# Mean norms: TensorE adds the last tile's sum and square, the mean is spread in two products, and GpSimd makes weight pieces ahead of rescaled tiles

## The reference

```python
def layer_norm(x, g, b):
    mu = jnp.mean(xf, axis=-1, keepdims=True)
    var = jnp.mean(jnp.square(xf - mu), axis=-1, keepdims=True)
    return (xf - mu) * lax.rsqrt(var + LN_EPS) * g + b

# second_block, l = 0, 1
h = modulate_2(x, sh1, sc1)
y = short_conv_mixer(h, ...) if l == 0 else forgetting_attention(h, ...)
x = layer_norm(DEEPNORM_ALPHA * x + g1 * y, ln1_g[l], ln1_b[l])    # n4 (l = 0), n6 (l = 1)
h = modulate_2(x, sh2, sc2)
y = swiglu(h, w_gate[l], w_up[l], w_down[l])
x = layer_norm(DEEPNORM_ALPHA * x + g2 * y, ln2_g[l], ln2_b[l])    # n5 (l = 0), n7 (l = 1), the output
```

## Time and profile before

| what | us |
|---|---|
| three runs: median (lowest to highest) | 1933.12 (1932.42 to 1933.66) |
| the profiled execution | 1932.42 |
| its span, first to last instruction | 1930.6 |
| TensorE busy | 1875.5 (97%) |
| VectorE, ScalarE, GpSimd busy | 1407.1, 853.5, 438.7 |
| mean granted TensorE clock | 0.992 of full |

### The profile page before, as it was taken

How to read it: one execution, slowest core, us unless ns; L and a number is a source line. 1 busy time by engine, 2 the same in 40 slices (tenths; PEclk the granted TensorE clock), 3 DMA queues, 4 the chain that set the end, 5 groups by cost and what they waited for, 6 DMA issues and landing times.

```text
span 1930.6 us, 25635 instructions
## 1 busy us (share of the span) xinstructions
PE 1875.5 (97%) x10248; PEld 1614.1 (84%) x10248; DVE 1407.1 (73%) x2157; ACT 853.5 (44%) x1296; POOL 438.7 (23%) x379
## 2 busy tenths in 40 slices
PE   6999999999999999999999999999999999999997
PEld 4788888878888887888789999977899778999996
DVE  7777665567766766776768787986677776877797
ACT  5677532352222225222534333457677553433343
POOL 4323111021111113001411121135634141112212
PEclk9999999999999999999999999999999999999998
DMA  9622366357667652753232323313221322332331
GB/s 333 163 81 72 127 220 239 109 197 260 242 241 258 242 194 62 297 187 130 67 105 94 107 89 109 110 66 135 67 66 44 98 77 89 108 107 91 109 100 54
DMA packets 142632, 267.76 MB, mean 139 GB/s; under 512 B 4576, under 2 KB 66032, under 8 KB 142513
## 3 DMA queue, kind: packets, MB, share of 16 engines
q1 hardware_dynamic: 137552, 248.59, 38.0%
q0 software_dynamic: 4960, 17.53, 2.6%
HBM read 261.84 MB, written 8.45 MB: 140 GB/s over the span
## 4 chain that ended last, share of the span: by engine, by line
PE 67%; DVE 5%; ACT 3%; POOL 2%; issue 2%; DVEq 0%; POOLq 0%; ACTq 0%
PE ps L739 21%; PE ps L741 21%; PE ps L740 21%; DVE t L1746 1%; DVE t L1798 1%; PE ps L899 1%; ACT t L1366 1%; ACT t L1362 1%; DVE t L1734 1%; PE ps L888 1%; PE ps L877 0%; POOL t L2630 0%; PE ps L916 0%; PE ps L917 0%; PE ps L915 0%
## 5 line engine op out<-in xcount | busy, mean ns | idle before, releaser
L739 PE MATMUL ps<-t 128*128 128x512 f32 (+1 forms) x2936 | 1026.3, 350 | 11.5 <-POOL t L2514 5.1
L741 PE MATMUL ps<-t 128*128 128x512 f32 (+1 forms) x2936 | 1020.1, 347 | 0.0
L740 PE MATMUL ps<-t 128*128 128x512 f32 (+1 forms) x2936 | 1016.6, 346 | 0.0
L739 PEld LDWEIGHTS ps<-t 128*128 128x128 f32 x2936 | 555.7, 189 | 85.0 <-issue 11.0
L741 PEld LDWEIGHTS ps<-t 128*128 128x128 f32 x2936 | 555.2, 189 | 72.1
L740 PEld LDWEIGHTS ps<-t 128*128 128x128 f32 x2936 | 555.5, 189 | 68.6 <-issue 1.0
L1734 DVE TENSOR_TENSOR t<-t 128x2048 fp32r<-128x2048 f32 x97 | 229.5, 2366 | 174.4 <-ACT t L1313 174.4
L1313 ACT ACTIVATE t<-t 128x2048 fp32r<-128x2048 f32 x97 | 185.3, 1910 | 328.6 <-PE ps L741 322.3
L1798 DVE SCALAR_TENSOR_TENSOR t<-ps,t 128x512 f32<-128x512 f32 x184 | 130.0, 746 | 68.1 <-PE ps L741 64.6
L1746 DVE CUSTOM_DVE_ANT_0 t<-t 128x1024 f32<-128x1024 f32 x144 | 168.8, 1220 | 3.6 <-DMA t<-in_ada 3.6
L2419 POOL TENSOR_TENSOR t<-t 128x512 fp32r<-128x512 f32 x88 | 115.4, 1329 | 195.1 <-ACT t L1320 194.4
(11 more groups left out here) (192 smaller groups left out, 1982.5 us busy)
## 6 DMA issues: line engine op xcount, KB each, us to landing
t<-in_ada SPq DMA_DIRECT2D x48, 1024.0 KB, 6.0
t<-in_gate SPq DMA_DIRECT2D x22, 1024.0 KB, 5.3
t<-in_up SPq DMA_DIRECT2D x22, 1024.0 KB, 5.3
t<-in_down SPq DMA_DIRECT2D x22, 1024.0 KB, 5.0
t<-in_w_in SPq DMA_DIRECT2D x17, 1024.0 KB, 6.2
t<-in_w_mlp_in SPq DMA_DIRECT2D x16, 1024.0 KB, 5.4
t<-in_w_mlp_out SPq DMA_DIRECT2D x16, 1024.0 KB, 5.1
t<-in_ada_t POOLq DMA_DIRECT2D x13, 1024.0 KB, 6.3
```

The source lines that it names most:

```text
L739: pe.matmul(o, wh, xh, start=first, stop=False)
L740: pe.matmul(o, wh, xl, start=False, stop=False)
L741: return pe.matmul(o, wl, xh, start=False, stop=last)
```

## The change

In each mean norm `sum7` and the addition of the last square are gone from VectorE. TensorE does both by accumulation: the products of `dsum` (tiles 0 to 6) and of tile 7 go to the same bank, and so do those of `acc` and of tile 7's square. The mean is spread by one product of `dsum` and one of tile 7 in bank 4 instead of 7. The centring of tile 0 moves ahead of the variance, so that two are left behind the reciprocal (in n7 three of four). In n5 the convert that stood ahead of the variance is cut in halves, one of them moved ahead of residual 6. In n3, n4 and n6 GpSimd's loop is split in two: the four pieces, then the eight rescaled tiles.

```diff
-                    on.wait_ge(acc, "dsum", site)
+                    on.wait_ge(p_sum, "dsum", site, 6)
                     for i, c in enumerate(blocks):
-                        ins = pe.matmul(psum[1][:, i:i + 1], m["dsum"][:, c], ones[:, 0:1], start=True, stop=True)
+                        pe.matmul(psum[1][:, i:i + 1], m["dsum"][:, c], ones[:, 0:1], start=i == 0, stop=False, ...)
+                    claim(4)
+                    pe.matmul(d[:, :], ones, m["dsum"], start=True, stop=False)
+                    on.wait_ge(acc, "acc", site, 6)
+                    for i, c in enumerate(blocks):
+                        pe.matmul(q[:, i:i + 1], m["acc"][:, c], ones[:, 0:1], start=i == 0, stop=False, ...)
+                    on.wait_ge(x_res, *last)
+                    for i, c in enumerate(blocks):
+                        ins = pe.matmul(psum[1][:, i:i + 1], X[7][:, c], ones[:, 0:1], start=False, stop=True, ...)
                     ins.then_inc(mm.sem, mm.up(site, "means"))
-                    on.wait_ge(acc, "acc", site, 7)
+                    pe.matmul(d[:, :], ones, X[7], start=False, stop=True).then_inc(mm.sem, mm.up(site, "mean"))
+                    on.wait_ge(a_norm, site, "sq", 7)
                     for i, c in enumerate(blocks):
-                        ins = pe.matmul(q[:, i:i + 1], m["acc"][:, c], ones[:, 0:1], start=True, stop=True)
+                        ins = pe.matmul(q[:, i:i + 1], m["sq"][0][:, c], ones[:, 0:1], start=False, stop=True, ...)
                     ins.then_inc(mm.sem, mm.up(site, "sums"))
-                    claim(7)
-                    pe.matmul(d[:, :], ones, m["dsum"], start=True, stop=True).then_inc(mm.sem, mm.up(site, "mean"))
...
             def roots(site, layer, *x_done):
                 if layer:
+                    centre(site, 0, *x_done)
...
-            sum7("n4", "co", 7)
-            add("n4", 7)
-            roots("n4", True)
+            roots("n4", True, x_res, "co", 0)
...
+                            if f == 5 and k == 5 and slot[0] < len(SLOTS):
+                                convert_half(slot[0], 0)
...
                 if slot[0] < len(SLOTS):
-                    convert(slot[0])
+                    convert_half(slot[0], 1)
...
             for k in range(KT):
                 next_piece(k)
+            for k in range(KT):
                 rescale("n4", "h4", k, cC, cD)
```

More of the change, by code:

```diff
@@ L821, in idle_products, with norm_finish @@
                     pe.matmul(psum[6][:, 0:256], ident, cst[:, 0:256], start=True, stop=True)
-            def norm_finish(site, layer, acc, rs_last):
+            def norm_finish(site, layer, acc, rs_last, *last):
                 m = norm_mem[site]
-                q, d, r = psum[3], psum[7], psum[5]
+                q, d, r = psum[3], psum[4], psum[5]
                 idle = site != "n1"
@@ L831, in norm_finish @@
                     claim(1)
-                    on.wait_ge(acc, "dsum", site)
+                    on.wait_ge(p_sum, "dsum", site, 6)
                     for i, c in enumerate(blocks):
-                        ins = pe.matmul(psum[1][:, i:i + 1], m["dsum"][:, c], ones[:, 0:1], start=True, stop=True)
+                        pe.matmul(psum[1][:, i:i + 1], m["dsum"][:, c], ones[:, 0:1], start=i == 0, stop=False,
+                                  skip_group_check=True)
+                    claim(4)
+                    pe.matmul(d[:, :], ones, m["dsum"], start=True, stop=False)
+                    on.wait_ge(acc, "acc", site, 6)
+                    for i, c in enumerate(blocks):
+                        pe.matmul(q[:, i:i + 1], m["acc"][:, c], ones[:, 0:1], start=i == 0, stop=False,
+                                  skip_group_check=True)
+                    on.wait_ge(x_res, *last)
+                    for i, c in enumerate(blocks):
+                        ins = pe.matmul(psum[1][:, i:i + 1], X[7][:, c], ones[:, 0:1], start=False, stop=True,
+                                        skip_group_check=True)
                     ins.then_inc(mm.sem, mm.up(site, "means"))
                     freed[1] = [(a_norm, (site, "squared"))]
-                    on.wait_ge(acc, "acc", site, 7)
+                    pe.matmul(d[:, :], ones, X[7], start=False, stop=True).then_inc(mm.sem, mm.up(site, "mean"))
+                    freed[4] = [(d_norm, (site, "centred", 7))]
+                    on.wait_ge(a_norm, site, "sq", 7)
                     for i, c in enumerate(blocks):
-                        ins = pe.matmul(q[:, i:i + 1], m["acc"][:, c], ones[:, 0:1], start=True, stop=True)
+                        ins = pe.matmul(q[:, i:i + 1], m["sq"][0][:, c], ones[:, 0:1], start=False, stop=True,
+                                        skip_group_check=True)
                     ins.then_inc(mm.sem, mm.up(site, "sums"))
-                    claim(7)
-                    pe.matmul(d[:, :], ones, m["dsum"], start=True, stop=True).then_inc(mm.sem, mm.up(site, "mean"))
-                    freed[7] = [(d_norm, (site, "centred", 7))]
                 else:
@@ L1167, in program_pe @@
             mm.also("end of h4")
-            norm_finish("n5", True, d_norm, "times")
+            norm_finish("n5", True, d_norm, "times", "dn", 0, 5, 7)
             at_end("pe", 5, mm)
@@ L1201, in program_pe @@
                         norm_shift("n6", 3, x_res, "op", 0)
-            norm_finish("n6", True, d_norm, "times")
+            norm_finish("n6", True, d_norm, "times", "op", 7)
             at_end("pe", 7, mm)
             ffn2(1, "n7", "h6")
-            norm_finish("n7", True, d_norm, "times")
+            norm_finish("n7", True, d_norm, "times", "dn", 1, 5, 7)
             at_end("pe", 8, mm)
@@ L1735, in convert, with convert_half @@
                     w_lo_d.sem, w_lo_d.up("slot", n))
+            def convert_half(n, half):
+                s = slice(1024 * half, 1024 * half + 1024)
+                on.wait_ge(w_hi, "slot", n)
+                ins = dve.tensor_tensor(WL[:, n % NW, s], raw[:, n % NRAW, s], WH[:, n % NW, s].bitcast(F), ALU.subtract)
+                if half:
+                    ins.then_inc(w_lo_d.sem, w_lo_d.up("slot", n))
             def ada_sum(j):
@@ L1822, in shift, with centre, roots @@
                         d_norm.sem, d_norm.up(site, "shifted", k))
-            def roots(site, layer):
+            def centre(site, k, *x_done):
+                on.wait_ge(mm, site, "mean")
+                on.wait_ge(*x_done)
+                dve.tensor_tensor(X[k], X[k], psum[4][:, :], ALU.subtract).then_inc(
+                    d_norm.sem, d_norm.up(site, "centred", k))
+            def roots(site, layer, *x_done):
                 v = col4[:, 0:4]
                 if layer:
+                    centre(site, 0, *x_done)
                     on.wait_ge(a_norm, site, "squared")
@@ L1841, in normed @@
             def normed(site, name, layer=False, tm=None, x_before=None):
[L1842 to L1846, removed]
                 if layer:
-                    for k in range(3):
-                        centre(k)
+                    for k in (1, 2):
+                        centre(site, k, *x_before(k))
                 on.wait_ge(mm, site, "rs")
@@ L1864, in normed @@
                     if layer and k + 3 < KT:
-                        centre(k + 3)
+                        centre(site, k + 3, *x_before(k + 3))
                     if name and k:
@@ L2394, in program_dve @@
             ffn2(1, "n7", 96, "n6", None)
[L2396 to L2403, removed]
+            for k in (1, 2, 5):
+                centre("n7", k, x_res, "dn", 1, 5, k)
             on.wait_ge(a_norm, "n7", "rs")
@@ L2408, in program_dve @@
                 if ahead:
-                    centre(ahead)
+                    centre("n7", ahead, x_res, "dn", 1, 5, ahead)
         def program_pool(pool, on):
```

15 lines of the change are left out of this document (3 added, 12 removed).

## The result

| | before | changed |
|---|---|---|
| runs: median (lowest to highest), us | 1933.86 (1932.42 to 1934.19) | 1942.16 (1941.27 to 1946.67) |
| the profiled execution, its span, us | 1932.42, 1930.6 | 1946.67, 1944.9 |
| mean granted TensorE clock | 0.992 | 0.987 |

A forecast was written before the change was run, and what follows sets the result against it. TensorE was taken to bound the kernel, with 67% of the chain. Norms and GpSimd's pieces in n3 to n7 plus 0.8 us for the clock gave +8.0 us, so 1941.1 us, range 1936.5 to 1945.5.

The forecast's parts named there:

- TensorE's list: In norms n4 to n7: with the added products, the variance comes 6.95 us behind the start of the idle products.
- What it gives back: In n4: the first normed tile follows the variance by 1.97 us instead of 2.69, which returns 0.72 us.
- GpSimd's tail: In n4 and n6: eight rescaled tiles behind the pieces take 8.55 us, so each norm costs +1.85 us.
- a wait at the third slot: In n4: TensorE waits about 1 us for VectorE's convert, 11 us later; no such wait would be wrong.
- The rival that kept the tail covered: Behind the norms: rescaled tiles run near 0.76 us and TensorE's own path counts; +5.4 us, 1938.5 us, chance 0.15.
- The price of the parts together: GpSimd's pieces ahead of the rescaled tiles: -0.2 us in n3, and 1.85 against 2.2 us in n4 and n6.
- The gain of the waits: TensorE's three waits for GpSimd's last piece go: 1.25 us gained in n4, 0.6 to 0.7 each in n3 and n6.
- The clock: In the four mean norms: more one-column products bring more falls to the 1.2 GHz level, +0.8 us together.
- The bound: In each mean norm: the most that falls of the clock were taken to cost, up to 1 us.
- The sum: Whole kernel: -0.2 (n3) + 1.85 (n4) + 1.4 (n5) + 1.85 (n6) + 2.3 (n7) + 0.8 (clock) = +8.0 us.
- One-column passes nearly free: Rival, in the mean norms: a one-column pass costs less than 0.05 us; -5 us, 1928 us, chance 0.05.

The follow-up runs named there:

- the second profile: The whole change run once more, unaltered, beside the kernel before: 1941.90 us against 1933.48, ratio 1.0046.
- The two wide kernels: The change, and separately the kernel before, each with the norms' one-column products streaming 128 columns: 1937.06 us, ratio 1.0022, and 1931.98 us, ratio 0.9992.

## Why the prediction was right

The direction, the time and the main mechanism held. Two terms of the sum were wrong, in opposite directions, and one of them by its mechanism too: that the total came out at 8.0 against 8.3 us is in part luck.

*TensorE's list.* Right: 6.95 us were forecast from the idle products to the variance, 6.75 are measured in n4 (934.53 - 927.78) at the full clock, with no wait of TensorE in between. What it gives back was right too: 1.97 us were taken from the variance to the first normed tile, 1.95 are measured in n5 of the second profile, all of it at the full clock. The two wide kernels show this term alone. From the idle products to the next slot the change costs +2.1 us in n4, +1.3 in n5 and +2.4 in n6 (10.55 in each, against 8.44, 9.23 and 8.17), and +2.0 in n7 from the idle products to the kernel's end. The forecast had +2.2, +1.4, +2.2 and +2.3.

*GpSimd's tail.* The step that failed. I took 3 x 1.20 + 5 x 0.99 = 8.55 us for the eight rescaled tiles, and from that a wait at the third slot of n4 and n6, which the forecast itself named as a sign of being wrong if it was missing. They take 7.39 us and there is no wait. The 0.99 was misread. It is the mean of four tiles, "beside a quiet VectorE", but one of these ran beside a busy one and took 1.72; the other three took 0.77. With 0.77 for the last five the same sum gives 3 x 1.20 + 5 x 0.77 = 7.45, and then the wait is gone from the forecast as well. The rival that kept the tail covered was right on this point. The price of the parts together was forecast as -0.9 us (-0.2 in n3, and 1.85 - 2.2 in each of n4 and n6); measured, the pieces bring -1.9 alone, -3.9 in the kernel before with wide products, and -4.0 with the changed norms. The gain of the waits was put too high in its turn: 0.7 of the 2.3 us come back as waits for VectorE's low halves, which the forecast did not have.

*The clock.* Named, with its cause, and mis-sized. I took +0.8 us over the kernel before. The wide products take some 4.3 us off the changed kernel and 0.8 off the kernel before, so the change brings about 3.5 us of falls. The bound was 1 us a norm; a short fall costs that (11.5 against 10.6 in the table), but one of about 10 us costs 3.5 (14.1 against 10.6), and in n4 to n6 of the kernel before there was none of that length. I had argued that the present norms show little, but the list was to be made longer in just the part that brings the falls on.

*The sum.* Without the clock the forecast had 7.2 us; with wide products in both kernels the change costs 4.0 + 0.8 = 4.8. With 0.8 against 3.5 for the clock the two errors nearly cancel. The split is not sharp, as each of these medians has an interval of about 1.8 us to either side.

*One-column passes nearly free.* Refuted in every profile: at the full clock 0.80 to 0.92 us for eight in each group. As 128 columns take about the same, it is not the streaming that sets the pace. The Trainium skill ("TensorE: Matmul & The Clock Gate", section "LDWEIGHTS (loading the stationary operand)") gives columns / 1.2 ns for a weight load, an estimate of 0.86 us for eight loads of 128 columns, and the 0.80 to 0.92 us lie around it. No run here changes the size of the load, so that it sets the pace is not shown apart from this.

## What to carry to other kernels

When work moves from one engine to another, compare with what each of them stands in front of: here VectorE had time to spare and TensorE was what all waited for, so two additions of 0.69 us on VectorE, of which 0.64 us stood on the path, became a variance that comes 2.7 us later. A pass of one column cost as much here as one of 128, and brought falls of the clock with it; streaming 128 columns of the same constant cost 0.1 us a norm and kept the clock up. Making next what is waited for next (pieces ahead of rescaled tiles) pays only if the end of the other work is still covered. To judge that, look at the single durations in a merged row and not at their mean, and at what the other engines did meanwhile.

## What the runs showed of the hardware

At the 2.4 GHz level eight float32 passes with a weight load each take 0.80 to 0.92 us when they stream one column and 0.86 to 0.99 when they stream 128; with one column at the 1.2 GHz level they take 1.71 us. With one-column groups in the norms the clock fell in 16 of 21 norms n4 to n6, for up to about 10 us and in different norms in different executions of one kernel; with 128-column groups in their place it did not fall in any of the 15 norms n4 to n6 of the five profiles made so. GpSimd's 128 x 512 scale-and-add takes 0.77 us while VectorE has nothing to do; the median of all 32 in the kernel before is 1.20. VectorE's subtraction of 128 x 1024 takes 2.33 us when it starts while a GpSimd addition runs, and 1.21 to 1.22 in the same kernels without one.
